# Casts, clears and masks of a two-block kernel in another order, and sums over heads in pairs

## The reference, cut to what matters

```
xs = h[None] + xx[None] * mu[:, None, None, :]
r, k, v = jnp.einsum('pbtd,pde->pbte', xs[:3], w_rkv)
...
w = -jax.nn.softplus(-(w0 + jnp.tanh(xw @ w1) @ w2)) - 0.5
...
a = jax.nn.sigmoid(a0 + (xa @ a1) @ a2)
g = jax.nn.sigmoid(xg @ g1) @ g2
...
kk = heads(k * k_k)
kk = kk / jnp.maximum(jnp.sqrt(jnp.sum(kk * kk, -1, keepdims=True)), 1e-12)
k = k * (1 + (a - 1) * k_a)
...
bonus = jnp.sum(rh * kh * r_k.astype(f32), -1, keepdims=True) * vh
```

## Time and profile before

| what | value |
|---|---|
| median of three runs | 2842.15 us |
| lowest and highest | 2839.92 and 2848.01 us |
| the profiled execution, its own time | 2859.77 us |
| its span in the trace | 2858.0 us |
| PE busy | 2611.4 us (91%) |
| DVE busy | 2057.1 us (72%) |
| ACT busy | 980.9 us (34%) |
| POOL busy | 393.1 us (14%) |

### The profile page before, as it was taken

The page is one execution under the profiler, slowest core; times in us unless marked ns, Lnnn a source line. Parts: engine busy times, 40 slices in busy tenths (PEclk is TensorE's granted clock), DMA queues, the critical chain, the costliest instruction groups (busy, mean ns, idle before and its releaser), DMA issues. The chain is left out here.

```text
span 2858.0 us, 43183 instructions
## 1 busy us (share of the span) xinstructions
PE 2611.4 (91%) x17344; PEld 2030.7 (71%) x17344; DVE 2057.1 (72%) x2802; ACT 980.9 (34%) x1056; POOL 393.1 (14%) x210
## 2 busy tenths in 40 slices
PE   5899888788999989998899996999898999999993
PEld 3674788546888854574788885897667788888882
DVE  6772576788777547645877757785865799999994
ACT  2531111122221013332122103333321677777772
POOL 1000000100000001000000000000001266666651
PEclk8998999999999989999999998999898999999997
DMA  5220222316664262201566422331216699999973
GB/s 194 77 81 10 82 91 77 134 52 191 180 190 138 96 212 95 74 31 51 178 187 180 147 96 95 96 97 59 105 43 232 220 369 370 375 368 364 362 303 133
DMA packets 247812, 459.65 MB, mean 161 GB/s; under 512 B 31125, under 2 KB 205869, under 8 KB 232313
## 3 DMA queue, kind: packets, MB, share of 16 engines
q1 hardware_dynamic: 227736, 433.74, 43.7%
q0 software_dynamic: 14256, 23.72, 2.4%
q10 hardware_dynamic: 5682, 0.20, 0.1%
HBM read 457.09 MB, written 30.56 MB: 171 GB/s over the span
## 5 line engine op out<-in xcount | busy, mean ns | idle before, releaser
L49 PE MATMUL ffn_bank<-ffn_xT_high,ffn_wi_high 128*128 128x512 f32 x704 | 279.6, 397 | 10.1 <-DVE ffn_wi_low L43 5.7
L50 PE MATMUL ffn_bank<-ffn_xT_low,ffn_wi_high 128*128 128x512 f32 x704 | 277.9, 395 | 0.0
L409 DVE SCALAR_TENSOR_TENSOR ffn_nsum<-ffn_nw,ffn_cond,ffn_nsum 128x256 f32<-128x256 f32 x336 | 163.0, 485 | 12.0
L49 PEld LDWEIGHTS ffn_bank<-ffn_xT_high,ffn_wi_high 128*128 128x128 f32 x704 | 133.7, 190 | 41.2 <-DVE ffn_wi_low L43 6.6
L3202 POOL DMA_INDIRECT expert_rows<-exp_ys,exp_to_row x32 | 155.9, 4871 | 45.1 <-issue 44.3
L50 PEld LDWEIGHTS ffn_bank<-ffn_xT_low,ffn_wi_high 128*128 128x128 f32 x704 | 133.4, 189 | 28.4
L43 DVE TENSOR_TENSOR moe_u_low<-moe_u,exp_u_high 128x4096 fp32r<-128x4096 f32 x32 | 141.6, 4425 | 13.5 <-ACT exp_u_high L3276 13.4
L43 DVE TENSOR_TENSOR moe_g_low<-moe_g,moe_g_high 128x4096 fp32r<-128x4096 f32 x32 | 141.7, 4428 | 9.3 <-ACT moe_g_high L3276 9.1
L49 PE MATMUL ffn_bank<-ffn_wo_high,ffn_act_high 128*128 128x512 f32 x352 | 138.6, 394 | 5.3 <-DVE ffn_wo_low L43 5.3
L43 DVE TENSOR_TENSOR moe_d_low<-moe_d,exp_d_high 128x4096 fp32r<-128x4096 f32 x32 | 141.4, 4418 | 0.0
L51 PE MATMUL ffn_bank<-ffn_xT_high,ffn_wi_low 128*128 128x512 f32 x352 | 139.5, 396 | 0.0
(11 more groups left out here) (690 smaller groups left out, 6585.4 us busy)
## 6 DMA issues: line engine op xcount, KB each, us to landing
moe_g<-in_w_e_gate SPq DMA_DIRECT2D x32, 2048.0 KB, 9.2
moe_u<-in_w_e_up SPq DMA_DIRECT2D x32, 2048.0 KB, 9.2
moe_d<-in_w_e_down SPq DMA_DIRECT2D x32, 2048.0 KB, 9.1
ffn_nw<-in_ada_w SPq DMA_DIRECT2D x24, 1024.0 KB
ffn_nw<-in_w_ada SPq DMA_DIRECT2D x24, 1024.0 KB
stay_z<-in_ffn_w_in SPq DMA_DIRECT2D x44, 512.0 KB, 5.2
ffn_wi<-in_ffn_w_in SPq DMA_DIRECT2D x44, 512.0 KB, 5.2
ffn_wo<-in_ffn_w_out SPq DMA_DIRECT2D x44, 512.0 KB, 3.5
```

The lines of the kernel that those rows point to most:

```text
L49: nc.tensor.matmul(out, w[0], x[0], start=start, stop=False, **kw)
L50: nc.tensor.matmul(out, w[0], x[1], start=False, stop=False, **kw)
L409: nc.vector.scalar_tensor_tensor(out=total, in0=nw[:, b, k, :], scalar=cond[:, k:k + 1], in1=total, op0=ALU.mult, op1=ALU.add).then_inc(s[ ...
```

## The change

It has six parts.

- **Quarters.** On ACT the cast of quarter 2 moves from behind step 5 of the exponentials to behind step 1, that of quarter 3 from behind the last shift to behind step 5. On DVE the low half of quarter 2 moves from behind step 5 of the rates to ahead of the loop, that of quarter 3 from behind receptance 4 to behind step 6 of the loop.
- **Sums.** Two sums are issued together (`pair_sums`): the even slice to output partitions 0 to 31, the odd one to 32 to 63, each with 32 columns of the selector. They stand behind K2, K4, K6 and V0, and behind V9, V11, V13 and V15, and wait for both squares. `squared` and the bonus parts on DVE wait for whole pairs. The norms, their inverses and the bonus now lie in 64 partitions, and `head_rows` is 64 x 1024 instead of 16 x 1024.
- **Bonus.** Its transposes move from behind G0 to behind Hg0; the copy at the end is two copies, one for even and one for odd slices.
- **Transposes behind Hg1.** Ten 128 x 128 transposes of the identity (`keep_busy`, L54) are added there; nothing reads what they write.
- **Masks.** They move to a buffer that outlives the first stage and are loaded in that stage on POOL's queue, once the input has been scaled (h_done).
- **Clears.** `Room.clear` collects semaphores, and only behind the stages mixed, ffn0, ffn1 and hyb does it place the two barriers and the clear.

```diff
+USED = []
+CLEARED_AFTER = ("mixed", "ffn0", "ffn1", "hyb")
+
+
 class Room:
...
-        if self.sems:
+        USED.extend(self.sems)
+        if self.sems and self.phase in CLEARED_AFTER:
             self.nc.all_engine_barrier()
-            self.nc.clear_and_free_semaphores(self.sems)
+            self.nc.clear_and_free_semaphores(USED)
             self.nc.all_engine_barrier()
+            USED.clear()
...
 QUARTER = D // 4
+SUM_ROWS = 64
 HALF_P = P // 2
...
-def rwkv_project(nc, room, buf, stay, x_in, cond_in, ada_w, ada_b, w, ident_dram, head_rows_dram):
+def rwkv_project(nc, room, buf, stay, x_in, cond_in, ada_w, ada_b, w, ident_dram, head_rows_dram, masks_dram):
...
     vec = room.sb("vec", [P, 6, KD])
-    head_of = room.sb("head_of", [P, KD, HEADS])
-    nrm, inv_low, bonus = room.shared(("nrm", [HEADS, T], F32), ("inv_low", [HEADS, T], F32R), ("bonus", [HEADS, T], F32))
-    inv_high = room.sb("inv_high", [HEADS, T], F32R)
+    head_of = room.sb("head_of", [P, KD, SUM_ROWS // 2])
+    nrm, inv_low, bonus = room.shared(("nrm", [SUM_ROWS, T], F32), ("inv_low", [SUM_ROWS, T], F32R), ("bonus", [SUM_ROWS, T], F32))
+    inv_high = room.sb("inv_high", [SUM_ROWS, T], F32R)
     resets = room.sb("resets", [P, T])
-    head_rows, hid = room.shared(("head_rows", [HEADS, D], F32R), ("hid", [P, 2, T], F32))
+    head_rows, hid = room.shared(("head_rows", [SUM_ROWS, D], F32R), ("hid", [P, 2, T], F32))
     kk, sq = (stay["z"][:, n * 2 * T:(n + 1) * 2 * T].rearrange("p (a t) -> p a t", a=2) for n in range(2))
-    head_rows_raw = stay["z"][0:HEADS, 0:D]
+    head_rows_raw = stay["z"][0:SUM_ROWS, 0:D]
     W0, A0, KK, KA, RK, KA1 = range(6)
...
             pool.dma_start(head_rows_raw, head_rows_dram).then_inc(selector_loaded, 16)
+            pool.wait_ge(h_done, KD)
+            pool.dma_start(buf["masks"][:, :, :], masks_dram).then_inc(buf["masks_loaded"], 16)
...
+            def pair_sums(into, q):
+
+                for odd in range(2):
+                    n = q + odd
+                    rows = slice(odd * SUM_ROWS // 2, (odd + 1) * SUM_ROWS // 2)
+                    last = nc.tensor.matmul(into[rows, :], head_of[:, n, :], sq[:, odd, :], start=(q == 0), stop=(q == KD - 2), skip_group_check=True)
+                return last
+
             def norm_sums(q):
-                pe.wait_ge(sq_done, q + 1)
-                nc.tensor.matmul(bank[5][0:HEADS, :], head_of[:, q, :], sq[:, q % 2, :], start=(q == 0), stop=(q == KD - 1),
-                                 skip_group_check=True).then_inc(sums_done, 1)
+                pe.wait_ge(sq_done, q + 2)
+                pair_sums(bank[5], q).then_inc(sums_done, 2)
...
             def head_sums(q):
-                pe.wait_ge(rk_done, q + 1)
-                nc.tensor.matmul(bank[6][0:HEADS, :], head_of[:, q, :], sq[:, q % 2, :], start=(q == 0), stop=(q == KD - 1),
-                                 skip_group_check=True).then_inc(rk_used, 1)
+                pe.wait_ge(rk_done, q + 2)
+                pair_sums(bank[6], q).then_inc(rk_used, 2)
...
                 last.then_inc(job_done, 1)
-                if name == "K" and q >= 1:
-                    norm_sums(q - 1)
+                if name == "K" and q >= 2 and q % 2 == 0:
+                    norm_sums(q - 2)
                 if (name, q) == ("V", 0):
-                    norm_sums(KD - 1)
+                    norm_sums(KD - 2)
                 if name == "V" and 7 <= q < 7 + KD:
                     spread_inverse(q - 7)
-                if name == "V" and q >= 4 * NT - KD:
-                    head_sums(q - (4 * NT - KD))
-                if (name, q) == ("G", 0):
+                if name == "V" and q >= 4 * NT - KD and q % 2:
+                    head_sums(q - (4 * NT - KD) - 1)
+                if (name, q) == ("Hg", 1):
+                    keep_busy(nc, bank[4], ident, 10)
+                if (name, q) == ("Hg", 0):
                     pe.wait_ge(bonus_done, 1)
                     for t in range(NT):
-                        last = nc.tensor.transpose(bank[7][:, t * HEADS:(t + 1) * HEADS], bonus[:, t * P:(t + 1) * P], ident[0:HEADS, 0:HEADS])
+                        last = nc.tensor.transpose(bank[7][:, t * SUM_ROWS:(t + 1) * SUM_ROWS], bonus[:, t * P:(t + 1) * P], ident[0:SUM_ROWS, 0:SUM_ROWS])
                     last.then_inc(bonus_psum, 1)
...
                 nc.scalar.activation(KT[:, q, :], AR[:, q, 0, :], ACT.Identity, bias=vec[:, KA1, q:q + 1], scale=vec[:, KA, q:q + 1]).then_inc(exps_done, 1)
+                if q == 1:
+                    quarter_high(2)
                 if q:
...
                 if q == 5:
-                    quarter_high(2)
+                    quarter_high(3)
             shift(KD - 1)
-            quarter_high(3)
             act.wait_ge(selector_loaded, 16)
...
                 if q >= 2:
-                    act.wait_ge(sums_done, q - 1)
+                    act.wait_ge(sums_done, q // 2 * 2)
                 nc.scalar.activation(sq[:, q % 2, :], kk[:, q % 2, :], ACT.Square).then_inc(sq_done, 1)
...
             act.wait_ge(sums_done, KD)
-            nc.scalar.activation(nrm[:, :], bank[5][0:HEADS, :], ACT.Sqrt).then_inc(root_done, 1)
+            nc.scalar.activation(nrm[:, :], bank[5][0:SUM_ROWS, :], ACT.Sqrt).then_inc(root_done, 1)
             for j in range(1, 4 * NT):
...
             act.wait_ge(rk_used, KD)
-            nc.scalar.copy(bonus[:, :], bank[6][0:HEADS, :]).then_inc(bonus_done, 1)
+            nc.scalar.copy(bonus[:, :], bank[6][0:SUM_ROWS, :]).then_inc(bonus_done, 1)
             for q in range(2):
...
             act.wait_ge(bonus_psum, 1)
-            nc.scalar.copy(BON[:, :, :].rearrange("p t h -> p (t h)"), bank[7][:, 0:NT * HEADS]).then_inc(bonus_turned, 1)
+            rows = bank[7][:, 0:NT * SUM_ROWS].rearrange("p (t a b o e) -> p t a b o e", t=NT, a=2, o=2, e=2)
+            for odd in range(2):
+                turned = nc.scalar.copy(BON[:, :, :].rearrange("p t (b o e) -> p t b o e", o=2, e=2)[:, :, :, odd, :], rows[:, :, odd, 0:KD // 2, odd, :])
+            turned.then_inc(bonus_turned, 1)
...
+            quarter_low(2)
             for q in range(KD):
...
                     receptance(q - 1)
-                if q == 5:
-                    quarter_low(2)
+                if q == 6:
+                    quarter_low(3)
             for q in range(3, KD - 1):
...
                         mix_one(V_xs, 1, k)
-                if q == 4:
-                    quarter_low(3)
                 if q == 6:
...
                 if q >= 2:
-                    dve.wait_ge(rk_used, q - 1)
+                    dve.wait_ge(rk_used, q // 2 * 2)
                 nc.vector.scalar_tensor_tensor(out=sq[:, q % 2, :], in0=AR[:, q, 1, :], scalar=vec[:, RK, q:q + 1], in1=KT[:, q, :],
...
         "BON": room.sb("BON", [P, NT, HEADS]), "cond": room.sb("cond", [P, KD]),
+        "masks": room.sb("masks", [P, LEVELS + 4, CHUNK]), "masks_loaded": room.sem("masks_loaded"),
     }
...
-    return np.repeat(np.eye(HEADS, dtype=np.float32), HD, axis=1)
-
-
-def rwkv_chunks(nc, room, buf, Y, acc, stay, ada_w, ada_b, masks_dram):
+    rows = np.zeros((2, SUM_ROWS // 2, HEADS, HD), dtype=np.float32)
+    for h in range(HEADS):
+        rows[h // 2 % 2, h, h] = 1.0
+    return rows.reshape(SUM_ROWS, D)
+
+
+def rwkv_chunks(nc, room, buf, Y, acc, stay, ada_w, ada_b):
...
-    masks = room.sb("masks", [P, LEVELS + 4, CHUNK])
+    masks = buf["masks"]
     ident = stay["ident"]
...
         def _(sp):
-            sp.dma_start(masks[:, :, :], masks_dram).then_inc(s["loaded"], 16)
             for n in range(2 * KD):
...
-            pe.wait_ge(s["loaded"], 16)
+            pe.wait_ge(buf["masks_loaded"], 16)
             for t in range(NT):
...
-            dve.wait_ge(s["loaded"], 16)
+            dve.wait_ge(buf["masks_loaded"], 16)
             for t in range(NT):
...
         with ExitStack() as inner:
-            rwkv_project(nc, Room(nc, inner, "proj"), buf, stay, x_in, cond_in, ada_w, ada_b, w, ident_dram, head_rows_dram)
+            rwkv_project(nc, Room(nc, inner, "proj"), buf, stay, x_in, cond_in, ada_w, ada_b, w, ident_dram, head_rows_dram, masks_dram)
         Y = Room(nc, ctx, "rwkv").sb("Y", [P, NT, D])
...
         with ExitStack() as inner:
-            rwkv_chunks(nc, Room(nc, inner, "chunks"), buf, Y, acc, stay, ada_w, ada_b, masks_dram)
+            rwkv_chunks(nc, Room(nc, inner, "chunks"), buf, Y, acc, stay, ada_w, ada_b)
```

2 lines of the change are left out of this document (1 added, 1 removed).

## The result

| | before | changed |
|---|---|---|
| median | 2842.0 us | 2822.2 us |
| lowest and highest | 2839.9 and 2848.0 | 2820.9 and 2827.3 |
| the profiled execution | 2859.8 | 2827.3 |
| mean granted clock in it | 0.951 | 0.958 |

The ratio is 0.9932 with an interval from 0.9917 to 0.9947: some 20 us gained, where 37 were forecast. The time lies at the upper end of the range, 0.2 us outside it. The two profiled executions, though, are 32.4 us apart in time and in span: the one of before lies 17.8 us above its median, the one of the changed kernel 5.1. That disagreement between trace and median is the first thing to read, and it is where the forecast fell.

A forecast was written before the change was run, and what follows sets the result against it. PE, busy nearly without a break from 104 to 288 us, was taken as the bound; 6.6 + 7.75 + 14.0 - 0.2 + 3.3 - 0.5 + 6.4 = 37.35 us off the median 2842.15 gave 2804.8 us, range 2799 to 2822.

The forecast's parts named there:

- Sum: Whole program: gains total 37.35 us, taken from both the median 2842.15 (giving 2804.8) and the profiled 2859.8 us (giving 2822).
- the G term: G jobs at the projection stage's end: filling PE's hole before them keeps full clock, gaining 14.0 us, at worst 0.
- Gain 14.0 us: Seven G jobs go from 4.03 to 2.02 us each if the clock stays up; at worst 0.
- G falls back all the same: G jobs: hole filled, but their stream still lets the clock fall; gain 23.35 us, time 2818.8 us; chance 0.30.
- The wait in front of R6: Projection stage: PE waits 2.3 us before job R6 for the later low half of weight quarter 3.
- The lower bound: Moved quarter casts: gain only 4 us instead of 6.6 if the 2.3 us before R6 pulls the clock down.
- The sign given for K0: New trace, phase K: K0's first reader at 128 to 129 us; beyond 131 the forecast is wrong.
- The pairs don't overlap: Paired sums over heads in K and V run in turn, losing 7.75 us: 2812.6 us; chance 0.05.
- the wait behind V0: Sum behind V0: PE waits 0.9 us for the square that ends at 184.81 us.
- Slower: Hole before R6 leaves PE at 0.50 through K and V, costing up to 100 us: about 2900 us; chance 0.01.
- the quarters give their gain back: Later rate steps make DVE late at R6 and K0, clock falls at both: 2810 to 2812 us; chance 0.07.

The follow-up runs named there:

- e10: Kernel before with two spare 1.9 us casts on ACT ahead of the second Hg sigmoid, lengthening PE's wait before G0; 2864.6 us.
- e11: Kernel before with the same two spare casts, the wait filled by 42 identity transposes and the bonus transposes behind Hg 0; 2844.8 us.
- e8: The changed kernel once more, with no edit, beside a run without the ten transposes; 2819.5 us.

## Why the prediction was wrong, point by point

- **The base.** The step that failed first is in "Sum": the difference of 17.6 us between the profiled execution and the median was seen, called an offset, and taken from both kernels alike. It was the very loss that the G term was to recover. By its time, the median of before had no slow G jobs in it: 2859.8 less 19.6, the distance of the two groups, is 2840.2, close to the median.
- **The G jobs.** The term that failed is "Gain 14.0 us": it is 0 of the median. What happens in the profiled execution was read rightly, and the rival "G falls back all the same" fell: a filled hole keeps the clock, the copies are 2.1 us apart (2.02 forecast), and the stream neither loses the clock from above nor regains it from below (e10, e11). But most executions of before lose nothing at this hole. The worth of the part, if filling the hole ends all the slow executions, is in the mean: 12 of 100 some 20 us above the rest, an estimate of 2.4 us. The question that was not asked is in how many executions the hole costs the clock.
- **Quarters.** 6.6 us forecast, 6.0 and 7.6 measured. The wait in front of R6 came as worked out (2.3 forecast, 2.55 in the trace), and K0 starts 48.9 us behind R0 (49.2 forecast). The lower bound had it that a fall of the clock at R6 costs up to 2.6 us; it fell in eight of nine traces and cost nothing, because K0 waits for DVE in any case. The sign given for K0, its reader at 128 to 129 us, failed (130.54, and 129.74 in e8): the reader hangs on DVE, not on K0's end, as the forecast had assumed.
- **Sums.** The pairs overlap fully (1.17 us a pair, 1.2 forecast), so the rival "The pairs don't overlap" is out, and the wait behind V0 is there (0.71, 0.9 forecast). 7.05 forecast, 6.8 when taken out, 1.7 alone, 5.8 and 6.2 in the traces. The larger selector costs somewhat more than the 0.5 us forecast: R0 starts at 73.84 to 74.88 in the nine traces that have it (74.4 in the mean) and at 73.22 to 73.95 in the nine without (73.55), 0.8 us apart.
- **Masks.** 3.3 us at their place, by the traces; between 0.4 and 5.6 in the medians. The forecast missed that the new semaphore gives the room `rwkv` a clear where the old clears stand.
- **Clears.** 6.4 forecast, 3.4 and 9.6 measured in medians, 5.7 by the boundaries of the traces. A boundary alone is cheaper (0.28 us) than the 0.45 worked out, so a clear costs more there, 1.09 us at the first boundary; the tail gives 1.9 us (1.8 forecast). Three boundaries with a merged clear then cost 1.4 us more together, for which the forecast had nothing.
- **Slower** and **the quarters give their gain back** did not occur: where the clock fell behind the wait at R6 it came back, and K0 started as early as was worked out.

Without the G term the sum gave 2842.15 - 23.35 = 2818.8 us, the number of the rival "G falls back all the same"; the changed kernel has 2822.2 in the first measurement and 2819.5 in the second. The number of that rival was nearly right, but by luck: its reason was not.

## What to carry to other kernels

Before a stall or a slow stretch of one trace enters a sum, compare the profiled execution with the median: where it is slower by about as much as the stretch costs, the stretch is probably the difference, and removing it changes the mean and the worst case but not the median. Take a second trace of the same kernel, which is the cheapest way to find out. And an edit that makes PE's stream continuous is worth judging by how many executions lie in the upper group, for which a median of a few runs is blind. Where the medians of small parts scatter by more than the parts are worth, compare the place of one instruction behind the edit in two traces: here that gave each part to about 1 us, where the medians were off by up to 4.
